# Order of the differential groups: frame stages 0 to 2, the sample, then frame stage 3

## What is computed

```python
def diff_attention(q, k, v, mask, lam, subln_g, lam_init):
    s = jnp.einsum('...qhcd,...khcd->...hcqk', q, k).astype(jnp.float32) * ATTN_SCALE
    s = jnp.where(mask, s, -jnp.inf)
    p = jax.nn.softmax(s, axis=-1)
    w = p[..., 0, :, :] - lam * p[..., 1, :, :]
    o = jnp.einsum('...hqk,...khe->...qhe', w.astype(v.dtype), v)
    return rms_norm(o, subln_g) * (1.0 - lam_init)
```

## Time and profile before

| | |
|---|---|
| median of three runs | 3062.81 us |
| the profiled execution | 3064.61 us, its span 3062.8 us |
| TensorE / VectorE / ScalarE / GpSimd busy | 90% / 51% / 38% / 12% of the span |
| TensorE's mean granted clock over the span | 0.942 |
| the differential phase | from 837.8 to 1352 us of the span |

### The profile page before, as it was taken

One profiled execution on the slowest core, in us unless ns is written; L12 is line 12 of the kernel. 1 busy time (PEld: TensorE's weight loads), 2 busy tenths in 40 slices (PEclk: granted clock), 3 DMA queues, 4 the chain that ended last, 5 costly groups with the idle time before them and its releaser, 6 DMA issues. The chain is left out here.

```text
span 3062.8 us, 54590 instructions
## 1 busy us (share of the span) xinstructions
PE 2747.4 (90%) x20536; PEld 1698.7 (55%) x20536; DVE 1555.3 (51%) x2976; ACT 1156.2 (38%) x1995; POOL 374.5 (12%) x465
## 2 busy tenths in 40 slices
PE   0999998377689999958988999999999999999998
PEld 0666665244466677734545565555656556565564
DVE  6555554476679988744542414334142342424326
ACT  2344444466568888853432111211112111121113
POOL 0122221100014555530000000000000000000001
PEclk9999999576669999989998999999999999999999
DMA  4344443111141100122212011010100101011002
GB/s 176 113 164 161 160 164 124 51 47 44 45 81 36 33 9 22 36 76 95 91 49 74 0 41 34 7 41 0 41 12 29 41 0 41 0 41 41 0 14 113
DMA packets 137938, 179.91 MB, mean 59 GB/s; under 512 B 60658, under 2 KB 100562, under 8 KB 136818
## 3 DMA queue, kind: packets, MB, share of 16 engines
q1 hardware_dynamic: 137842, 178.61, 18.0%
HBM read 133.92 MB, written 42.17 MB: 57 GB/s over the span
## 5 line engine op out<-in xcount | busy, mean ns | idle before, releaser
L1984 ACT ACTIVATE silu<-gate_ps,scales 128x352 f32<-128x352 f32 x132 | 73.3, 556 | 1141.2 <-PE up_ps L2024 1141.2
L1915 DVE SCALAR_TENSOR_TENSOR act<-up_ps,scales,silu 128x352 f32<-128x352 f32 x132 | 77.1, 584 | 779.3 <-ACT silu L1984 779.3
L2022 PE MATMUL gate_ps<-ffn_inT_hi,gate_hi 128*128 x1056 | 331.3, 314 | 15.4 <-DVE up_lo L1903 15.4
L1927 DVE SCALAR_TENSOR_TENSOR residual_rows<-down_ps,scales,residual_rows 128x512 f32<-128x512 f32 (+1 forms) x374 | 278.8, 748 | 118.4 <-PE down_ps L2034 117.4
L2024 PE MATMUL gate_ps<-ffn_inT_hi,gate_lo 128*128 x1056 | 331.1, 314 | 0.0
L2023 PE MATMUL gate_ps<-ffn_inT_lo,gate_hi 128*128 x1056 | 331.1, 314 | 0.0
L2024 PE MATMUL up_ps<-ffn_inT_hi,up_lo 128*128 x1056 | 330.0, 313 | 0.0
L2023 PE MATMUL up_ps<-ffn_inT_lo,up_hi 128*128 x1056 | 330.0, 313 | 0.0
L2022 PE MATMUL up_ps<-ffn_inT_hi,up_hi 128*128 x1056 | 330.0, 313 | 0.0
L2032 PE MATMUL down_ps<-down_hi,act_hi 128*128 128x512 f16 (+1 forms) x748 | 283.8, 379 | 0.0
L2033 PE MATMUL down_ps<-down_lo,act_hi 128*128 128x512 f16 (+1 forms) x748 | 283.5, 379 | 0.0
(11 more groups left out here) (271 smaller groups left out, 5651.1 us busy)
## 6 DMA issues: line engine op xcount, KB each, us to landing
w_scan<-in_w_gate SPq DMA_DIRECT2D x16, 704.0 KB, 6.8
w_scan<-in_w_up SPq DMA_DIRECT2D x16, 704.0 KB, 8.1
w_scan<-in_w_down SPq DMA_DIRECT2D x16, 704.0 KB, 4.0
gate<-in_w_gate SPq DMA_DIRECT2D x22, 512.0 KB, 6.0
up<-in_w_up SPq DMA_DIRECT2D x22, 512.0 KB, 7.3
down<-in_w_down SPq DMA_DIRECT2D x22, 512.0 KB, 3.3
keys_values<-in_w_in SPq DMA_DIRECT2D x8, 1152.0 KB, 15.2
x_tile<-in_x SPq DMA_DIRECT2D x17, 512.0 KB, 3.4
```

Source lines behind the costliest of these rows:

```text
L1927: nc.vector.scalar_tensor_tensor(H[0:rows, at:at + 512], YP[(2 * t + n) % 4][0:rows, :], SC[0:rows, S_YI:S_YI + 1], H[0:rows, at:at + 512] ...
L2022: nc.tensor.matmul(out, FH[w][:, k, c], nh, start=k == 0, stop=False)
```

## The change

The stages come in the order F0, F1, F2, sample, F3. As a frame stage is first now, its start is split: q of the first head alone (`q_first`), then the keys of the sample, the low parts, the keys of F0, the constant rows, and then the other heads' q. The keys of F1, F2 and F3 are copied in three transfers. The scores of each frame stage wait for its own keys, those of the sample for none, as its keys are waited for in F0's count of 48. `seen` starts at -1, so that TensorE waits for the other heads' q at the first piece behind unit 0. The planner's code is otherwise as before, and works on the new order.

```diff
--- before.py
+++ after.py
@@ -1009,6 +1009,9 @@
 POOL_FULL = (0, 1, 2)
 
 
+STAGE_ORDER = (0, 1, 2, NT // 4, 3)
+
+
 class Unit:
 
     def __init__(self, k, g, c, kind, blocks, rows, parts, cols, buf):
@@ -1075,7 +1078,7 @@
 
 
     def __init__(self):
-        order = [NT // 4] + list(range(NT // 4))
+        order = STAGE_ORDER
         self.groups = [Group(4 * s + h, s, n, h) for s, n in enumerate(order) for h in range(HDIF)]
         self.units, self.first, self.last = [], [], {}
         users = {}
@@ -1210,9 +1213,10 @@
              "pool_p_lo", "av", "recip_step", "o_out", "squares", "square_sum", "mean_square", "rstd", "normed", "consts",
              "w_out_scanned"))
         stored = [s("stored0"), s("stored1")]
+        q_first = s("q1_first_head_in")
         q_in = [s(f"q1_in{n}") for n in range(2)]
         ql_in = [s(f"ql_in{n}") for n in range(2)]
-        k2_in = [s(f"k2_in{n}") for n in range(3)]
+        k2_in = [s(f"k2_in{n}") for n in range(NT // 4)]
         wo_in = [s(f"w_out_in{n}") for n in range(2)]
         vt = lambda V, t, h, rows: V[rows, (t * HDIF + h) * VW:(t * HDIF + h + 1) * VW]
         w_out = dram["w_out"].rearrange("a m d -> (a m) d")
@@ -1227,12 +1231,13 @@
         with nc.Block() as block:
             @block.sync
             def _(sp):
-                def load_q1(stage):
+                def load_q1(stage, heads=slice(0, HC), done=None):
                     gr = groups[4 * stage]
                     for q in range(gr.nq):
                         r = (gr.tile0 + q) * P
-                        sp.dma_start(Q1[stage % 2][:, :, q * P:(q + 1) * P],
-                                     g.q1[r:r + P, HS * P:].rearrange("p (h n) -> p h n", n=P)).then_inc(q_in[stage % 2], 16)
+                        sp.dma_start(Q1[stage % 2][:, heads, q * P:(q + 1) * P],
+                                     g.q1[r:r + P, (HS + heads.start) * P:(HS + heads.stop) * P].rearrange("p (h n) -> p h n", n=P))\
+                            .then_inc(done or q_in[stage % 2], 16)
 
                 def load_ql(stage):
                     gr = groups[4 * stage]
@@ -1244,16 +1249,18 @@
                 def copy_keys(n, a, b):
                     sp.dma_start(K2[0:HD, :, a * P:b * P], K1[0:HD, :, a * P:b * P]).then_inc(k2_in[n], 16)
 
-                load_q1(0)
+                load_q1(0, slice(0, 2), q_first)
+                copy_keys(0, NT, NKT)
                 load_ql(0)
-                copy_keys(0, NT, NKT)
+                copy_keys(0, 0, 4)
                 sp.wait_ge(mrow_ok, 1)
                 sp.dma_start(K2[HD:HD + 2, :, :].rearrange("p h n -> p (h n)").rearrange("p (m n) -> p m n", n=P),
                              CM[:, :].unsqueeze(1).broadcast_to([2, HC * NKT, P])).then_inc(k2_in[0], 16)
+                load_q1(0, slice(2, HC))
                 load_q1(1)
                 load_ql(1)
-                copy_keys(1, 0, 4)
-                copy_keys(2, 4, NT)
+                for n in range(1, NT // 4):
+                    copy_keys(n, 4 * n, 4 * n + 4)
 
                 def store(gr):
                     sp.wait_ge(f_ok, gr.index + 1)
@@ -1473,8 +1480,8 @@
                         pe.wait_ge(q2_out, gr.index + 1)
                     if u.k in plan.stage_first:
                         stage = plan.stage_first.index(u.k)
-                        if stage < 3:
-                            pe.wait_ge(k2_in[stage], 32 if stage == 0 else 16)
+                        if gr.frame:
+                            pe.wait_ge(k2_in[gr.n], 48 if gr.n == 0 else 16)
                     hc = 2 * gr.h + u.c
                     for t, at, q, n in u.blocks:
                         out = SP[u.k % 2][:, at:at + n * P]
@@ -1502,13 +1509,13 @@
                                                     stop=u.k == plan.last[gr.index, u.c], skip_group_check=True)
                     last.then_inc(av_ok, 1)
 
-                pe.wait_ge(q_in[0], q_loads(0))
+                pe.wait_ge(q_first, 16 * groups[0].nq)
                 for p in plan.pieces[0]:
                     max_piece(p)
                 q2T(groups[0])
                 scores(units[0])
                 scores(units[1])
-                seen = 0
+                seen = -1
                 for k in range(K + LAG):
                     if k + 2 < K:
                         scores(units[k + 2])
```

## The result

The changed kernel took 3114.45 us (median of five runs, 3109.06 to 3114.94) against 3063.81 us for the kernel before in the same series. The ratio is 1.016, with a 95% interval of 1.0146 to 1.0174: slower by 1.6%, or 50.6 us. Forecast were 3095 us, 1.0% slower, and a range that ended at 3112. The direction and the mechanism were right; the sizes of most terms were not. Between the two spans, 3113.1 us (the profiled execution of the changed kernel, 3114.9) and 3062.8, lie 50.3 us, 18.4 more than the forecast sum of 31.9. The measured median lies 2.5 us above the range.

What follows compares the result with a forecast made beforehand. The bound was taken to differ by stage: TensorE in sample and F2, VectorE in F0 and F1, ScalarE with TensorE in the last group. Terms summed to +31.9 us on 3064.6; less 1.8 for the median, 3095 us, range 3077 to 3112.

Steps and rivals of the forecast that it cites:

- the start: Before the first exponent: 1872 KB at 158 GB/s take 12.1 us, first exponent at 852 instead of 849.55, +2.5 us.
- F0: First frame stage: 1.5 us waiting for the other heads' q and 5 more pieces at 0.68 us on VectorE, +4.9 us.
- F2: Third frame stage: 28 pieces less at 0.235 us each, -6.6 us.
- the sample: Sample's stage before F3: 3.5 + 1.5 + 40 + 19 = 64 us against 28.6, +35.4 us.
- F3: Last stage: 27 pieces less give back 6.3 us, first units at the lower clock cost 2 us.
- The planner's list and the block: At unit 196 the planner places 57 pieces at once, on the path, at 0.70 us each: 40 us.
- the 28 units: Units of the sample's stage behind the block: 19 us, from 5.4 us for each 8.
- The price of a piece beside a unit: In F2, one piece beside a unit costs 1.404 - 1.17 = 0.235 us, with 1.17 taken from the last group.
- F3's cold start: F3's first units may run at the lower clock: +2 us, at worst 6 us lost, at best nothing.
- Rival 2: The start is longer, SP standing blocked between its issues: about +10 us more, 3105 us; chance 0.10.
- the other heads' q: At unit 0 TensorE waits for this 768 KB, landing at 856.5 us; 1.5 us of the wait shows.
- the third rival: Lower clock throughout: block 43 us, the 28 units 24, F3's first 12 us at half speed, 3107 us; chance 0.16.

Runs made afterwards that it cites:

- The even placing: The changed kernel with the planner's target set back to what is done while the next piece may not be placed; 3088.05 us, ratio 1.0077 to before.
- the block in the old order: The kernel before, with F3's pieces not placed before unit 208 instead of 132, so 33 pieces stand at one unit; 3085.41 us, ratio 1.0075.

## Why the prediction was right, and where it was wrong

The mechanism was right, and five terms of the sum were too small a loss or too large a gain: the start, F0, F2, the sample and F3. They missed by 4.2, 2.9, 2.3, 3.1 and 6.2 us.

- **The planner's list and the block.** Right: unit 196, 57 pieces, VectorE without a pause that shows, ScalarE idle for 41.2 us, 39.6 us for the block (forecast 40). The even placing and the block in the old order show that it is the cause, and that it has its price anywhere. The 40 was partly luck. The forecast took 0.70 a piece as a middle between 0.63 at the full clock and 0.75 at the lower one. The block ran at 0.50 but for its first 2 us, and the round was 0.695 there, since the bank was free for the next matmul 0.06 us behind its reduce, not 0.15; at the full clock it was 0.60. Ahead of the block 5.4 us passed (forecast 5.0), with a wait of 1.4 us for q (1.5). Behind it the 28 units took 22 us, not 19, at a clock of 0.54.
- **The price of a piece beside a unit**, 0.235 us, was the step "one piece beside a unit thus costs 1.404 - 1.17". It measured 0.136. With that, F2 gives back 28 x 0.136 = 3.8 us, where 4.3 were measured and 6.6 forecast; and F3 3.7 instead of 6.3.
- **F3's cold start** was put at "+2", with 6 as its worst. F3 came out 1.9 us longer instead of 4.3 shorter. With 3.7 given back, its start cost some 5.6 us, at a clock of 0.57 over the first 16 us; its first group alone took 48.9 us against 45.4 before. Of F3's miss of 6.2 us, the largest of the sum, 2.6 are the price of a piece and 3.6 its start. It is also the term that differs from one execution to the next: in the traces of two variants with the same block F3 was 4.5 and 4.9 us shorter.
- **The start** was the step "1872 KB are 12.1 us": a mean rate over 30 us was used for a stretch that holds all of the constant rows' copy, 3 to 4 us at 19 to 26 bytes a ns. It was +6.7 instead of +2.5, just inside the bound of +7 given there. Rival 2 named the place and the direction; how much of the rest is SP standing at its issues wasn't separated.
- **F0** was +7.8 instead of +4.9. VectorE's own part, 53.8 - 49.7 = 4.1 us more work, is close to the forecast 3.4. The 1.5 us for the other heads' q didn't come: TensorE shows no wait for them. In its place VectorE was idle 3.5 us more, none of it in the first 12 us (2.6 against 2.7). Behind these it waited 4.3 us for the matmuls of pieces, against 1.6 before, at a clock of 0.80 against 0.93.
- **The reading of the earlier trace rows.** As said with the result, three of its rows are not first exponents. The lengths of F0, F1 and F3 in the prediction, 55.4, 95.4 and 181.9, are 58.6, 94.3 and 180.0. No term of the sum hangs on them.
- **The range.** The five terms missed on the same side; the range had been made as if some would fall short. Rivals 2 and 3, each with its own chance, both came true in part, and they add up: 10 and 12 us on the forecast would have been 3117. Two of the five runs, near 3109, lie inside the range; the median doesn't.
- The section of the Trainium skill that the prediction names (TensorE: Matmul & The Clock Gate, "HAM oscillation — how this bites in real kernels") is about bursts of matmuls with waits for transfers between them that are longer than the bursts. In the block TensorE's waits were 0.15 to 0.6 us, so the block doesn't test that rule, though it did run at the lower level, as the third rival had it (that rival's block was 43 us; 39.6 were measured). That wasn't free: it cost some 5 us in the block, and more behind it.

## What to carry to other kernels

A planner that paces work by a running target must not let the target run while the work may not be placed; otherwise the arrears fall due at one point, and what was hidden beside other work becomes a block on the path. Before stages are reordered, ask for each what must be ready for its successor and how much time it leaves for that: a short stage can't cover a long one's preparation. Take the price of an added instruction from two groups in the middle of a pipeline; the last group came out too short here, 1.17 us a unit against 1.28 to 1.31.

## What the runs showed of the hardware

- Reduces of 128x512 from PSUM, fed by one matmul each through two banks, started 0.60 us apart at clock 1.00 and 0.695 us apart at 0.50. Each took 0.68 to 0.69 us in both.
- In the block TensorE was shown busy 33.4 of 39.6 us, and was granted 0.52, the lower level for nearly all of it.
- A copy of 80 KB to two partitions in packets of 256 bytes drained at 19 to 26 bytes a ns, with a share of 0.12 to 0.20 of the engines, for 3 to 4 us, and what was queued behind it waited. With packets of 2 KB the wait at its end was as long (5.6 us against 5.4). A mean rate over the stretch hides it.
